# Where the forty late halves of the modulation projection are multiplied: a two-layer hybrid backbone on one core

## The reference, cut to what matters

```python
def modulation(cond, w, b):
    return jnp.split(jax.nn.silu(cond) @ w + b, 6, axis=-1)
for i in range(DEPTH):
    sh1, sc1, gt1, sh2, sc2, gt2 = modulation(c, mod_w[i], mod_b[i])
    csh1, csc1, cgt1, csh2, csc2, cgt2 = modulation(c_ctx, mod_w[i], mod_b[i])
    ...                                   # norm with sh1, sc1, then the mixer
    x = x + gt1 * m_lat
    x = x + gt2 * conv_ffn(modulate(rms_norm(x, norm_ffn_g[i]), sh2, sc2), ...)
```

## Time and profile before

| | us |
|---|---|
| median of 3 runs | 1561.51 |
| the runs | 1561.51, 1550.75, 1562.24 |
| the profiled execution | 1549.92 |
| its span | 1548.1 |
| PE busy | 1425.9 (92%) |
| DVE, ACT, POOL busy | 888.5, 599.4, 142.7 |
| granted TensorE clock, mean | 0.968 of full |

### The profile page before, as it was taken

One profiled execution on the slowest core, in us unless ns is written; L12 is line 12 of the kernel. 1 busy time (PEld: TensorE's weight loads), 2 busy tenths in 40 slices (PEclk: granted clock), 3 DMA queues, 4 the chain that ended last, 5 costly groups with the idle time before them and its releaser, 6 DMA issues. The chain is left out here.

```text
span 1548.1 us, 30846 instructions
## 1 busy us (share of the span) xinstructions
PE 1425.9 (92%) x13547; PEld 1192.7 (77%) x13547; DVE 888.5 (57%) x1268; ACT 599.4 (39%) x968; POOL 142.7 (9%) x153
## 2 busy tenths in 40 slices
PE   3798999899999799999999999989999999799998
PEld 2566677777887688777778888867887768799998
DVE  3559643545464455555556124787776665688844
ACT  2323544222231244333343114454543554455534
POOL 1000000233242030000000002000002330000000
PEclk8999989899999899999999999999999999899999
DMA  9321101144324132556652332222242004366643
GB/s 326 87 82 55 55 28 41 57 143 136 111 88 136 56 109 82 164 163 176 185 156 82 109 108 90 69 82 82 82 136 82 2 10 147 108 183 181 191 163 109
DMA packets 169744, 172.30 MB, mean 111 GB/s; under 512 B 15270, under 2 KB 135946, under 8 KB 169610
## 3 DMA queue, kind: packets, MB, share of 16 engines
q1 hardware_dynamic: 167216, 165.14, 34.8%
q0 software_dynamic: 1088, 4.19, 0.7%
q10 hardware_dynamic: 1306, 0.99, 0.2%
HBM read 169.26 MB, written 1.05 MB: 110 GB/s over the span
## 5 line engine op out<-in xcount | busy, mean ns | idle before, releaser
L315 DVE TENSOR_TENSOR w_lo<-w_raw,w_hi 128x2048 fp32r<-128x2048 f32 x95 | 216.1, 2274 | 213.6 <-ACT w_hi L305 213.5
L640 PE MATMUL bank<-h,w_hi 128*128 128x256 f32 (+2 forms) x968 | 333.5, 345 | 5.5 <-issue 2.9
L644 PE MATMUL bank<-h,w_lo 128*128 128x256 f32 (+2 forms) x968 | 324.8, 336 | 0.0
L643 PE MATMUL bank<-h,w_hi 128*128 128x256 f32 (+2 forms) x968 | 324.8, 336 | 0.0
L305 ACT ACTIVATE w_hi<-w_raw 128x2048 fp32r<-128x2048 f32 x95 | 180.3, 1898 | 198.2 <-PE bank L640 145.7
L658 DVE SCALAR_TENSOR_TENSOR acc<-bank,params,acc 128x510 f32<-128x510 f32 (+3 forms) x272 | 173.1, 645 | 86.2 <-ACT acc L1644 60.0
L640 PEld LDWEIGHTS bank<-h,w_hi 128*128 128x128 f32 (+1 forms) x968 | 185.6, 192 | 40.2 <-issue 22.6
L643 PEld LDWEIGHTS bank<-h,w_hi 128*128 128x128 f32 (+1 forms) x968 | 185.6, 192 | 20.1 <-issue 2.9
L644 PEld LDWEIGHTS bank<-h,w_lo 128*128 128x128 f32 (+1 forms) x968 | 185.4, 192 | 18.8
L1644 ACT ACTIVATE acc<-bank,params 128x512 f32<-128x512 f32 (+1 forms) x88 | 48.8, 580 | 152.4 <-PE bank L644 52.5
L640 PE MATMUL bank<-h_hi,w_hi_hyb 128*128 128x512 f32 (+1 forms) x184 | 77.2, 420 | 11.5 <-DVE dn_qkv L658 4.4
(11 more groups left out here) (416 smaller groups left out, 2834.5 us busy)
## 6 DMA issues: line engine op xcount, KB each, us to landing
w_raw<-in_ffn_up SPq DMA_DIRECT2D x88, 512.0 KB, 5.2
w_raw<-in_mod_w SPq DMA_DIRECT2D x40, 1024.0 KB, 5.3
w_raw<-in_ffn_down SPq DMA_DIRECT2D x22, 1024.0 KB, 4.8
w_raw<-in_ssm_w_in SPq DMA_DIRECT2D x20, 1024.0 KB, 5.2
w_raw<-in_hyb_w_in SPq DMA_DIRECT2D x9, 1024.0 KB, 5.1
w_raw<-in_ssm_w_out SPq DMA_DIRECT2D x8, 1024.0 KB, 4.7
mod_early<-in_mod_w SPq DMA_DIRECT2D x4, 1024.0 KB, 17.3
mod_early<-in_mod_w POOLq DMA_DIRECT2D x4, 1024.0 KB, 14.2
```

The lines of the kernel that those rows point to most:

```text
L315: dve.tensor_tensor(lo, raw, hi.bitcast(F32), ALU.subtract).then_inc(k.lo_done.sem, 1)
L640: mm = pe.matmul(out, wh, xh, start=(start and n == 0), stop=False)
L643: pe.matmul(out, wh, xl, start=False, stop=False)
L644: mm = pe.matmul(out, wl, xh, start=False, stop=(stop and n == last))
```

## The change

All forty late halves now stand in `stage_delta_solve`. The list gives iterations 0 to 4 two halves each, 5 and 6 three, 7 and 8 none, 9 to 12 three, 13 and 14 two, 15 and 16 none, 17 and 18 three, and 19 two. The batches become groups 0 to 3, 4 to 11, 12 to 19 and 20 to 23; their turns stand in iterations 7 and 15 and in the tail, with `mod_row` one iteration earlier and `mod_bias` one later. The FFN of layer 0 has no modulation, and the plan of loads has all late halves ahead of the loads of the output projection.

```diff
--- before.py
+++ after.py
@@ -334,7 +334,7 @@
     return slot.rearrange("p (k n) -> p k n", k=KD)[:, :, 0:width]
 
 
-MOD_BATCHES = ((0, 4), (4, 12), (12, 16), (16, 24))
+MOD_BATCHES = ((0, 4), (4, 12), (12, 20), (20, 24))
 
 
 def mod_batch(g):
@@ -1836,8 +1836,10 @@
         scan[3, n, 1] = (piece, 4)
 
     mods = {it: [] for it in range(NP * LV)}
-    for n, it in enumerate((0, 1, 2, 2, 3, 4, 5, 5, 6, 7, 8, 8, 9, 10, 11, 11, 14, 15, 16, 16, 17, 18, 18, 19)):
+    counts = (2, 2, 2, 2, 2, 3, 3, 0, 0, 3, 3, 3, 3, 2, 2, 0, 0, 3, 3, 2)
+    for n, it in enumerate(it for it, c in enumerate(counts) for _ in range(c)):
         mods[it].append(8 + n)
+    turns = {7: 1, 15: 2}
     tail = [(piece, s) for s in (5, 6, 7) for piece in ("ks", "w", "ds")]
     with ExitStack() as st:
         def sb(name, shape):
@@ -2025,8 +2027,8 @@
                         mm.then_inc(x_done.sem, 1)
                     for m in mods[it]:
                         mod_products(k, pe, m)
-                    if it == 12:
-                        mod_turn(k, pe, 1)
+                    if it in turns:
+                        mod_turn(k, pe, turns[it])
                     for l in range(2):
                         e = event(pi, lv, l)
                         un = ORDER[2 * pi + l]
@@ -2069,7 +2071,7 @@
             for n, (name, s) in enumerate(tail):
                 piece(name, s)
                 if n == 1:
-                    mod_turn(k, pe, 2)
+                    mod_turn(k, pe, 3)
 
         @block.scalar
         def _(act):
@@ -2111,8 +2113,8 @@
                         e = event(pi, lv, l)
                         act.wait_ge(x_done.sem, x_done.at(e + 1))
                         act.activation(Xm[:, l, :, :], v8(XY(l)[:, :]), ACT.Copy).then_inc(xc_done.sem, 1)
-                    if it == 11:
-                        mod_row(k, act, 1)
+                    if it + 1 in turns:
+                        mod_row(k, act, turns[it + 1])
                     for l in range(2):
                         name, s = scan.get((pi, lv, l), ("", 0))
                         if name == "ds":
@@ -2141,7 +2143,7 @@
                             o.act_high(act)
             for s in (5, 6, 7):
                 if s == 5:
-                    mod_row(k, act, 2)
+                    mod_row(k, act, 3)
                 out(s)
                 if s == 6:
                     split_hi(k, act, first)
@@ -2273,8 +2275,8 @@
                 more = pi < NP - 1
                 for lv in range(LV):
                     it = pi * LV + lv
-                    if it == 13:
-                        mod_bias(k, dve, 1)
+                    if it - 1 in turns:
+                        mod_bias(k, dve, turns[it - 1])
                     for l in range(2):
                         e = event(pi, lv, l)
                         un = ORDER[2 * pi + l]
@@ -2320,7 +2322,7 @@
                     o.dve_low(dve)
                 if (name, s) == ("ds", 6):
                     split_lo(k, dve, first)
-            mod_bias(k, dve, 2)
+            mod_bias(k, dve, 3)
 
     nl = NCH * LV
     for t, cnt in zip(k.tallies["di"], (NCH, NCH, NCH, NCH, NCH, NCH, NCH, nl, nl, nl, nl, nl, NCH, NCH, NCH, NCH, NCH, NCH, NCH, 1, 0)):
@@ -3023,7 +3025,7 @@
     with ExitStack() as st:
         row0 = RowGemm(k, 0, 2, g_out, 4, cat, 0, opens=True, out=out, parts=2)
         norm1 = PartNorm(k, 0, 1, row0, h[0], h[1], b, g_up)
-        up = FfnUp(k, 0, g_up, g_down[0], norm1, gh, gl, b.acc, mods=32, paired=True)
+        up = FfnUp(k, 0, g_up, g_down[0], norm1, gh, gl, b.acc, paired=True)
         down = RowGemm(k, 0, 5, g_down, KF // 2, lambda c: (gh(c), gl(c)), 0, up=up, parts=2)
         norm2 = PartNorm(k, 1, 0, down, h[0], h[1], b, g_ssm)
         ssm = SsmIn(k, a, g_ssm, norm2, b)
@@ -3222,10 +3224,10 @@
         k.stream.kinds["mod"] = len(k.mod_load)
         g_hyb = hyb_loads(k, a["hyb_w_in"][0])
         mod_loads(k, a["mod_w"][0], 4, 12)
-        mod_loads(k, a["mod_w"][1], 0, 4)
+        mod_loads(k, a["mod_w"][1], 0, 12)
         up0, ssm_in = (a[n][0].rearrange("(k p) n -> p k n", p=P) for n in ("ffn_up", "ssm_w_in"))
         g_out, ahead = att_row_loads(k, a["hyb_w_out"][0], [up_parts(up0, c) for c in range(2)])
-        g_up0 = pair_loads(k, a["ffn_up"][0], a["mod_w"][1], 4, first=ahead)
+        g_up0 = pair_loads(k, a["ffn_up"][0], first=ahead)
         g_down0, g_ssm = row_loads(k, a["ffn_down"][0], KF // 2, [[((0, 2 * P), ssm_in[:, :, c:c + 2 * P])] for c in (S_X, S_X + 2 * P)])
         g_ssm.append(len(k.stream.plan))
         k.stream.add("split", [((0, 2 * SH), a["ssm_w_in"][0].rearrange("(k p) n -> p k n", p=P)[:, :, S_DT:SSM_IN])])
```

## The result

| | before | after |
|---|---|---|
| median of 4 runs, us | 1558.69 | 1604.88 |
| lowest, highest | 1550.75, 1562.24 | 1601.33, 1606.57 |
| profiled execution | 1549.92 | 1603.46 |
| its span | 1548.1 | 1601.7 |
| mean granted clock | 0.968 | 0.948 |

The changed kernel takes 1.0304 times the time of the kernel before (95% interval 1.0271 to 1.0336), 46.2 us more by the medians. The forecast was +39.4 us and 1596 us.

The account below looks back on a forecast made before the run. PE was taken to bound both the up projection and the iterations. -20.9 + 14.5 + 35.2 + 13.6 - 3.0 = +39.4 us, so 1589.3 us against the profiled execution; forecast 1596 us, range 1574 to 1611.

Parts of the forecast that it names:

- The third half waits for its load: Iterations with three halves: PE waits 4.4 us for the third load in each of eight, 35.2 us.
- The clock: Behind each of the eight waits PE's clock falls to half rate: 1.7 us each, 13.6 us; bounds 0 and 26.4.
- The cheap rival: Iterations: clock holds and all issue gaps are swallowed; +21.6 us, 1571.5 us; chance 0.18.
- the costly one: Iterations: clock falls twice as long each time, nothing is swallowed; +55.2 us, 1605.1 us; chance 0.10.
- PE's work in the iterations: Iterations: PE's added halves 13.5 us and one more turn 1.0 us; sum +14.5 us.
- The FFN: Layer 0's FFN gets shorter: 16 halves 19.5 us, batch turn 0.8, bias wait 0.6; sum -20.9 us.
- the bias: Down projection: PE's wait for the fourth batch's bias goes, 0.6 us.
- What the waits give back: Iterations: other engines and PE's instruction supply catch up during waits, shrinking earlier gaps; 3 us taken, between 0 and 7.2.
- Two halves in successive iterations thus just fit: Iterations: load behind a second half lands at 469.3 us, next iteration's halves begin at 470.27, adding no wait.
- The rival on the other side: Three-half iterations: third load is there in time, only PE's work counts; -6.4 us, 1543.5 us; chance 0.07.

Follow-up runs that it names:

- Experiment 2: Kernel before, its 24 halves in the iterations put mostly in threes, nothing moved between the stages: 1587.48 us, ratio 1.0202.
- experiment 4: Changed kernel, each iteration's halves spread: first behind the X products, second and third in the first and second chunk's block: 1550.81 us, ratio 0.9957.
- experiment 1: Changed kernel, third halves placed behind the first chunk's Y and X products instead of directly behind the second half: 1582.82 us, ratio 1.0163.
- experiment 6: Changed kernel, loads of the eight third halves bring only 256 of 512 rows: 1587.45 us, ratio 1.0195.
- experiment 3: Changed kernel with five extra matmuls, results unused, ahead of each third half: 1586.64 us, ratio 1.0193.
- Experiment 5: Kernel of experiment 4, with iteration 9 at two halves and iteration 13 at three: 1547.31 us, ratio 0.9930.
- experiment 7: Against the changed kernel: 32 halves by twos in iterations 0-7 and 10-17, behind the X products, 8 in the FFN: 1563.42 us, ratio 1.0058.
- experiment 8: Kernel of experiment 7, each iteration's second half moved to the second chunk's block: 1552.88 us, ratio 0.9995.

## Why the prediction was right

**The third half waits for its load.** Right in place, number and size: eight waits, in the eight iterations named, 36.5 us against 35.2. Experiment 2 makes them in the kernel before, experiment 4 takes them away with all forty halves still in the iterations, experiments 1 and 6 shorten them by more cover and by a smaller load.

**The clock.** 13.6 us were charged. From the region: 65.1 - 14.5 (PE's work, as predicted) - 36.5 (waits) + 0.7 (issue gaps, 8.7 before and 8.0 after) = 14.8 us; the clock's share gives 16.9, and experiment 3, which fills the waits, is 17.4 us shorter in the region. So the step is right and its size too small, and that it came out so near is in part luck. 1.7 us for each wait stood for 3.4 us at 1.2 GHz, since dense work follows. Three of the eight waits have a stretch of that length behind them; the other five have 6.8 us, of which 5.4 to 6.0 fall on busy time. That is 2.4 us for each wait, 19 us in all, and about 2 us less than before were lost elsewhere in the region. Dense work thus did not decide the length, and what did is open. The cheap rival, in which the clock holds, is excluded by its mechanism; the costly one had the stretches right in five places of eight and is excluded by its size alone, +55.2 us where the interval ends at about +52. The Trainium skill, "TensorE: Matmul & The Clock Gate", section on HAM oscillation, had the same form, half rate behind each DMA wait, and the eight third halves at 1.93 us agree with it.

**PE's work in the iterations.** +14.5 us was not measured by itself. In the changed kernel it is 12.4 us or more, by the split above. Experiment 5 is a second look: its region is only 10.4 us longer than before with forty halves, one more turn and waits for loads of 0.4 us, but its clock was better, 0.99 against 0.95 over the region, and its waits for DVE were 2.9 us shorter. PE was busy 12.7 us longer, with 5.3 us at 1.2 GHz against 22.5; the work added lies between 12.7 and 21.3 us, where the prediction's prices give 17.6 for forty single entries and the turn. That agrees, and bounds no more.

**The FFN.** -19.5 - 0.8 were predicted for the slots and the turn, and the up projection got 20.5 us shorter; -0.6 for the bias, and the down projection got 0.7 us shorter. Right, with nothing late in its place.

**What the waits give back.** 3 us were put here and 0.7 us were found. The reason given, that PE's instruction supply catches up during a wait, holds only where the waits take the place of pairs of loads (experiment 2: 8.5 us); in the changed kernel the two-half iterations keep or enlarge their gaps. This and 2.5 us too little for the waits and the clock, less 1.3 us that the other stretches gave, are the miss of the sum: the touched stretches give +42.8 us (65.1 - 1.1 - 20.5 - 0.7), where +39.4 was predicted. The medians give +46.2; the 3.4 us between them no stretch explains.

**A sentence that was too narrow.** "Two halves in successive iterations thus just fit" was right for the slots of the ring: in experiment 7 no pair waited. But two loads in one piece have a price of their own, which I had not weighed and which cost experiment 7 its gain.

**The rival on the other side** said that the third load is there in time. In the changed kernel it never was; the kernels of experiments 4 and 5 are what it described, 0.4% and 0.7% faster than before, near its -6.4 us. The nearness is luck: forty single entries cost 3.1 us more than it had, by the same prices, and the clock's share was 6.8 and 8.6 us smaller than before, which it did not have. Why the clock falls less often in these kernels no run isolates.

## What to carry to other kernels

With a ring of n slots, only n loads can be used in one go on an in-order engine: put the next use at least one whole load time (here 1.1 us to release and issue and 5 us to land) behind the use that frees its slot, or every engine behind it stands. Count such a wait as its length plus what the clock loses behind it, here about 2 us for waits of 4.3 to 4.9 us. Before judging where work should be moved, try spreading it: the same move was 3% slower in clusters and 0.7% faster when spread.

## What the runs showed of the hardware

A wait of PE of 2.5 us costs less afterwards than one of 4.6 us, but not nothing: in experiment 1 the region is 44.2 us longer, of which 20.3 are waits and about 15.5 PE's work (14.5, and 0.13 us for each of eight more entries), so about 8 us, 1 us for each wait, are left for the clock and the rest. The clock's share gives 9.9 us (busy at 1.2 GHz: 42.4 us against 22.5), 1.2 us for each.

Two loads of 1 MB issued 0.9 us apart fill the DMA engines for about 6 us at 400 GB/s, and in 13 places of experiment 7 PE then stood for up to 3.3 us, mostly about 1.5, with no releaser; 4 to 7 us apart, in experiment 8, they cost half of that. The Trainium skill, "Runtime: NRT & Kernel Launch", section on instruction fetch, says that each engine's sequencer fetches its instructions by a DMA queue of its own and calls the cost of this mostly hidden. The trace agrees on the queue (q8, in packets of 16 KB), but beside 2 MB of weights in one piece the cost was not hidden here: PE went on only 1.2 to 1.6 us after a packet had landed, fourteen times, and experiments 7 and 8 differ by 10 us.
